# Expert gathers of a hybrid decoder step: the V stream issued 36 tiles behind the U stream in place of 32

## The reference, cut to what matters

```
q = (xb @ w_q).reshape(tb, 8 heads, 2, 128)
s = einsum('thpc,hpkc->thpk', q, sub_keys)      # 2 x 128 scores per token and head
sv, si = top_k(s, 16)                           # best 16 of each half
cv, ci = top_k(sum of all 16x16 pairs, 16)      # best 16 pairs per head
expert = i1 * 128 + i2                          # 8 x 16 = 128 experts per token
act = gelu(einsum('tkd,td->tk', expert_u[expert], xb))
y   = einsum('tk,tkd->td', softmax(cv) * act, expert_v[expert])
```

## Time and profile before

| what | value |
|---|---|
| median of three runs | 3461.09 us |
| the profiled execution's own time | 3466.26 us |
| its span, first to last instruction | 3464.5 us |
| PE matmul busy | 1794.1 us (52%) |
| DVE busy | 1980.7 us (57%) |
| ACT busy | 358.6 us (10%) |
| POOL busy | 1954.1 us (56%) |
| software DMA queue (POOL's gathers) | 1090.65 MB, 79.9% of 16 engines |

### The profile page before, as it was taken

One profiled execution on the slowest core, in us unless ns is written; L12 is line 12 of the kernel. 1 busy time (PEld: TensorE's weight loads), 2 busy tenths in 40 slices (PEclk: granted clock), 3 DMA queues, 4 the chain that ended last, 5 costly groups with the idle time before them and its releaser, 6 DMA issues.

```text
span 3464.5 us, 25701 instructions
## 1 busy us (share of the span) xinstructions
PE 1794.1 (52%) x7978; PEld 746.8 (22%) x7978; DVE 1980.7 (57%) x5165; ACT 358.6 (10%) x908; POOL 1954.1 (56%) x2091
## 2 busy tenths in 40 slices
PE   4499998434444444444444444444444444444444
PEld 3244443311111111111111111111121111112111
DVE  0121412776666666666666666666666666677761
ACT  0202101101001101101101010001000100011000
POOL 0000000377776776677667767776777677766644
PEclk7699999666666666666666666667666676676756
DMA  9500104599999999999999999999999999999977
GB/s 354 207 0 25 73 0 164 184 395 399 409 407 381 408 409 410 375 407 407 405 375 409 404 405 379 406 407 385 403 406 410 374 410 407 408 351 378 389 294 284
DMA packets 334185, 1169.71 MB, mean 338 GB/s; under 512 B 39222, under 2 KB 46150, under 8 KB 332008
## 3 DMA queue, kind: packets, MB, share of 16 engines
q0 software_dynamic: 298256, 1090.65, 79.9%
q1 hardware_dynamic: 29368, 73.60, 5.9%
q10 hardware_dynamic: 6432, 3.90, 0.4%
HBM read 1154.54 MB, written 13.48 MB: 337 GB/s over the span
## 4 chain that ended last, share of the span: by engine, by line
DMA 21%; DVE 20%; POOL 18%; PE 11%; issue 9%; ACT 3%; POOLq 0%; ACTq 0%; DVEq 0%
DMA v_rows<-in_expert_v_dram,v_idx 15%; POOL v_rows L1083 9%; PE ps_y L1458 9%; POOL wide L1076 5%; POOL u_rows L1076 4%; DVE wide L1325 4%; DMA wide<-in_expert_u_dram,u_idx 3%; DVE u_rows L1325 3%; DMA u_rows<-in_expert_u_dram,u_idx 2%; PE ps_a L1418 1%; DVE pick L1283 1%; DVE pick L1289 1%; DVE pick_f L1294 1%; ACT L1149 1%; DVE top_i L1248 1%
## 5 line engine op out<-in xcount | busy, mean ns | idle before, releaser
L1458 PE MATMUL ps_y<-v_rows,spread 128*32 128x512 f32 x4096 | 845.4, 971 | 1171.7 <-DMA v_rows<-in_expert_v_dram,v_idx 1154.7
L1083 POOL DMA_INDIRECT v_rows<-in_expert_v_dram,v_idx x1024 | 968.1, 945 | 453.0 <-issue 296.8
L1325 DVE CUSTOM_DVE_ANT_0 wide<-wide,ps_x 128x1024 f32<-128x1024 f32 x512 | 613.1, 1218 | 390.0 <-DMA wide<-in_expert_u_dram,u_idx 380.5
L1325 DVE CUSTOM_DVE_ANT_0 u_rows<-u_rows,ps_x 128x1024 f32<-128x1024 f32 x512 | 609.5, 1218 | 276.9 <-DMA u_rows<-in_expert_u_dram,u_idx 274.9
L1076 POOL DMA_INDIRECT wide<-in_expert_u_dram,u_idx x512 | 480.7, 939 | 210.9 <-issue 135.7
L1076 POOL DMA_INDIRECT u_rows<-in_expert_u_dram,u_idx x512 | 482.2, 942 | 192.6 <-issue 126.6
L1458 PEld LDWEIGHTS ps_y<-v_rows,spread 128*32 128x32 f32 x4096 | 165.2, 150 | 1581.6 <-issue 1555.2
L1402 PE MATMUL ps_a<-wide,h2T 128*128 128x256 f32 x1152 | 299.2, 417 | 8.6 <-ACT h2T L1118 6.4
L1402 PEld LDWEIGHTS ps_a<-wide,h2T 128*128 128x128 f32 x1152 | 236.4, 211 | 133.0 <-issue 90.1
L624 POOL DMA_DIRECT2D wide<-in_w_q_dram x1 | 1.1, 1077 | 393.4 <-PE mix_pair L794 393.4
L794 PE MATMUL mix_pair<-hT,wide 128*128 128x512 f32 x512 | 220.8, 593 | 0.0
(11 more groups left out here) (219 smaller groups left out, 1630.4 us busy)
## 6 DMA issues: line engine op xcount, KB each, us to landing
ada_w<-in_w_ada_dram SPq DMA_DIRECT2D x12, 2048.0 KB, 14.7
v_rows<-in_expert_v_dram,v_idx POOLq DMA_INDIRECT x1024, 8.0
wide<-in_w_in_dram SPq DMA_DIRECT2D x1, 10240.0 KB, 38.2
x_in<-in_x_prompt_dram SPq DMA_DIRECT2D x16, 512.0 KB, 4.2
wide<-in_w_q_dram POOLq DMA_DIRECT2D x1, 8192.0 KB, 23.6
wide<-in_expert_u_dram,u_idx POOLq DMA_INDIRECT x512, 8.0
u_rows<-in_expert_u_dram,u_idx POOLq DMA_INDIRECT x512, 8.0
h_in<-h_rows SPq DMA_DIRECT2D x9, 512.0 KB, 6.8
```

The source lines that it names most:

```text
L1083: pool.indirect_dma_start(v_rows[g % RING][:, :], None, t["expert_v"][0], bass.IndirectOffsetOnAxis(ap=idx, axis=0)).then_inc(v_landed[g % ...
L1325: dve.tensor_tensor_reduce(rows[:, :], rows[:, :], x, 1.0, 0.0, ALU.mult, ALU.add, acc).then_inc(done, 1)
L1458: last = pe.matmul(ps_y[32 * j:32 * j + 32, c * HALF:(c + 1) * HALF], spread[n % 2][:, 32 * m:32 * m + 32], v_rows[(g + j) % RING][:, c * ...
```

## The change

A constant `LAG = WIDE + 4 = 36` is added, and POOL's issue loop is written anew, as one loop over steps with a list of V tiles. U tiles keep their steps up to 1023. V tile j of the list is issued at step j + 36 in place of j + 32. The samples' eight U gathers move from steps 1024 to 1031 to steps 1028 to 1035, and with them the wait for the samples' indices. The order of the V tiles, the rings, and the programs of PE, DVE, ACT and SP stay the same.

```
+    LAG = WIDE + 4
+            v_tiles = [(n, i) for n in range(ROUNDS) for i in range(TILES)]
+            v_tiles[TILES // 2 - TILES:TILES // 2 - TILES] = [(ROUNDS, e) for e in range(NS)]
+            for step in range(len(v_tiles) + LAG):
+                n, i = divmod(step, WIDE)
+                if n < ROUNDS:
+                    if i == 0:
+                        pool.wait_ge(u_idx_ready, n + 1)
+                    gather_u(step, u_idx[n % KEPT][:, i:i + 1])
+                elif 0 <= step - TILES * (ROUNDS - 1) - LAG < NS:
+                    e = step - TILES * (ROUNDS - 1) - LAG
+                    if e == 0:
+                        pool.wait_ge(s_idx_ready, 4)
+                    gather_u(WIDE * ROUNDS + e, s_idx[:, e // 2, e % 2:e % 2 + 1])
+                if step >= LAG:
+                    n, i = v_tiles[step - LAG]
+                    if n == ROUNDS:
+                        gather_v(step - LAG, s_idx[:, i // 2, i % 2:i % 2 + 1])
+                    else:
+                        if i == 0:
+                            pool.wait_ge(v_idx_ready, n + 1)
+                            pool.wait_ge(gate2_done, 2)
+                        m = tile_at(i)
+                        gather_v(step - LAG, v_idx[n % KEPT][:, m:m + 1])
```

More of the change, by code:

```diff
@@ L1084, in gather_v @@
                                         bass.IndirectOffsetOnAxis(ap=idx, axis=0)).then_inc(v_landed[g % RING], 16)
-            for n in range(ROUNDS + 1):
-                for i in range(WIDE):
-                    if n < ROUNDS:
-                        if i == 0:
[L1090 to L1098, removed]
+            v_tiles = [(n, i) for n in range(ROUNDS) for i in range(TILES)]
[16 more added lines that the diff above has]
+                    else:
+                        if i == 0:
+                            pool.wait_ge(v_idx_ready, n + 1)
                             pool.wait_ge(gate2_done, 2)
                         m = tile_at(i)
[L1101 to L1105, removed]
+                        gather_v(step - LAG, v_idx[n % KEPT][:, m:m + 1])
         @block.scalar
```

## The result

The changed kernel takes 3935.41 us (median of four runs, 3927.88 to 3940.86) against 3462.74 us for the kernel before: ratio 1.136, 95% interval 1.1338 to 1.1383. It is slower, in the way that the prediction gave, by 473 us where 391 were forecast; the time lies 5.4 us above the upper end of the range. The profiled execution took 3927.88 us with a span of 3926.1, so the two traces differ by 461.6 us.

What follows compares the result with a forecast made beforehand. The DMA's gather rate was taken to bound the kernel, at 81.9 us a round. Rounds 1 to 27 +324, rounds 28 to 30 +62 and round 31 +7 made +393 us: 3854 us, range 3700 to 3930.

Steps and rivals of the forecast that it cites:

- The mechanism: DVE waits in order for scores hanging on later V tiles, closing loops through U buffers; POOL stands 7.5 and 9.7 us.
- late rounds: Rounds 28 to 30, with three searches each: 111.1 us a round in place of 90.53, +62 us.
- the landing time of the first loop: V gather of step 19 to quad 3, 6.8 us, within 21.2 us through search and product 17 to U gather 25.
- second ones: V gather of step 31 through landing (6.6 us), scores, search with softmax and product 29 to U gather 37: 23.4 us.
- the stretch of 29 gathers: From U gather 37 at step 37 to the V gather of step 51 (next round's step 19), at POOL's pace: 36.0 us.
- that of 13 gathers: From U gather 25 at step 25 to the V gather of step 31, at POOL's pace: 16.2 us.
- hole: At a block's second round POOL stands 8.07 us before V tile 8, for quad 0; the change was to remove it.
- The long end of the landing time: Gathers taking 8.0 us to land in place of 6.8 and 6.6: 99.4 us a round, 3938 us in all.
- the slack wins: Rival, chance 0.05: the hole's price falls away, searches stand no longer since PE's order limits scores; faster, 3384 us.
- Only one search is late: Rival, chance 0.06: the queue absorbs the standstill before U gather 25; 89.3 us a round, +160, 3621 us.
- Does not do what it says: Rival, chance 0.03: V gathers already stand at the ring's limit, so later issue lands nothing later; no change, 3461 us.
- The end: Round 31 from step 1000 to the samples' first gather: 102.0 us in place of 95.2, +7 us; its index wait below 30.89.

## Why the prediction was wrong in size and right in kind

*The mechanism holds.* What was to be seen is there: waits for the scores of about 13 us, two standstills in each round released by products 17 and 29, V tile 8 without a wait, the slices even. Moving the scores, the search, or the ring's end each undoes the loss (1.5% stays where the late rounds kept their order), and moving the scores alone makes it.

*The term that failed is the landing time of the first loop.* I took 6.8 us from issue to quad, from a V tile seven steps after a standstill, for a V gather that comes fourteen steps after one. In the changed kernel the 27 first loops have 8.0 us in the mean (6.6 to 10.4), and the 27 second ones, six steps after a standstill, 6.9 (I took 6.6). The loops measure 22.5 and 23.8 us where I had 21.2 and 23.4; the stretch of 29 gathers takes 36.7 in place of 36.0, that of 13 gathers 16.2 as worked out. Sum 99.1 in place of 96.8: 2.3 us a round, 63 us in 27 rounds, of the 69 by which the span outgrew the sum. The late rounds gave another 7 (113.5 in place of 111.1).

Where it comes from: POOL issues a gather in 1.24 us and the DMA moves one in 1.28, so the queue grows in a long stretch, by about a microsecond over 29 gathers (29 x 0.04). I had written that POOL is hardly faster, and not drawn it out to step 51. The trace of before shows the growth: in the flow of the earlier trace rows V tile 27, twelve steps after V tile 15 with its 6.68 us, took 7.52 us to land, which I passed over:

```profile
2128.95 7.52 DMA v_rows<-in_expert_v_dram,v_idx
```

Round 17 was also a poor round to take the term from, since its hole comes shortly before V tile 15: in the mean of rounds 1 to 27 of the kernel before, this tile took 7.5 us from issue to quad. In the changed kernel the landing time rises from 6.4 us at the sixth gather behind U gather 37 to 7.5 at the V gather of the first loop, in the mean of the 20 stretches into which no start of a block falls. The rest is SP's traffic. At the start of a block it loads and stores up to 1.5 MB between the gathers. In such a stretch of the changed kernel (1395 to 1420 us; count, median us to landing):

```profile
h_in<-h_rows SPq DMA_DIRECT2D x1, 512.0 KB, 7.3
out_y_prompt_dram<-out_rows SPq DMA_DIRECT2D x1, 512.0 KB
x_in<-x_rows SPq DMA_DIRECT2D x1, 512.0 KB
v_rows<-in_expert_v_dram,v_idx POOLq DMA_INDIRECT x8, 10.7
```

10.7 us. My sum had no such rounds in it. With the traffic cut, issue to quad in the first loops went from 8.0 to 7.8 us in the mean (from 9.4 to 7.9 in the first rounds of blocks), the stretch of 29 gathers from 36.7 to 36.2, and the total by 22 us. A round still takes 1.8 us more than my sum, of which 1.0 is the landing of the first loop; so the larger part is the growth of the queue, which I read from the landing times and did not test by itself.

*The range.* The long end of the landing time gave 3938 us in my own working; I gave 3930 and moved the lower end out instead. The traces differ by 461.6 us; that the medians differ by 11 more is the spread of the executions, since the profiled one was the fastest of the four after the change, and the slowest of those before.

*The rivals.* Of "the slack wins" the first half is true and the price was right in kind: the hole goes, and with the scores moved along, the rounds reach 83.7 us, not quite the DMA's 81.9. Its second half, that scores hang on PE's order and not on the tile, fell with the result: PE's program is the same, and DVE's waits for scores grew from 190.3 to 861.0 us. "Only one search is late" fell: both loops make POOL stand, 8.9 and 10.5 us in the mean, and with the first search mended the second still costs 8 us a round. "Does not do what it says" fell with the waits for quads, 154.6 to 50.5 us. The end was as worked out: the samples' first gather waited 28.11 us after 30.89, and step 1000 onwards gave the 6 us that I had as 7.

## What to carry to other kernels

When one of two interleaved streams is issued later, look for everything whose place was chosen by that stream's landing, here a third activity (the search) threaded between the two: shift it by the same distance, or the wait moves there. A wait costs nothing until a buffer ring closes it into a loop; count the issues between the loop's two ends, multiply by the pace, and set that against the loop's time. For a loop, take the landing time at that point of the queue's growth, and not right after a standstill.

## What the runs showed that I had not expected

The landing time of a 512 KB gather ranged from 4.2 us alone over 6.9 us six steps after a standstill to 10.7 us beside other transfers, at a nearly constant rate of issue. And twelve U buffers in place of eight, without moving the scores, brought the hole of the block's end back (7.22 us): more buffers for one stream let it run ahead of the engine that both streams wait for.
